# Two experts at a time, each in a piece of 2048 and a piece of 1536 columns, with the routing sums and the decay rows made in another way

## The chip, the cores and the metric

The kernel runs on one core of a Trainium2 chip. Its engines are TensorE (PE, with its weight loads listed apart as PEld), VectorE (DVE), ScalarE (ACT), GpSimd (POOL) and SyncE (SP), which here only issues the transfers of weights. The metric is the device time of one execution in microseconds; the median of three executions counts.

## The reference, cut to what matters

Two layers on 256 tokens of 1024 channels, all in fp32. Each layer mixes tokens in three ways (convolution, Mamba-2 state space, attention), then has a feed-forward part: dense in layer 0, eight experts of which each token takes two in layer 1.

```python
SEQ, D_MODEL, FFN_EXPERT, N_EXPERTS, MOE_TOPK = 256, 1024, 3584, 8, 2

def _swiglu(h, wg, wu, wd):
    return (jax.nn.silu(h @ wg) * (h @ wu)) @ wd

def _moe(h, router_w, router_b, wg, wu, wd):
    logits = (h @ router_w + router_b).astype(jnp.float32)
    top_v, top_i = lax.top_k(logits, MOE_TOPK)
    top_w = jax.nn.softmax(top_v, axis=-1)
    gates = jnp.sum(top_w[..., None] * jax.nn.one_hot(top_i, N_EXPERTS, dtype=jnp.float32), axis=-2)
    ...
    for e in range(N_EXPERTS):
        out = out + gates[..., e:e + 1] * _swiglu(h, wg[e], wu[e], wd[e])
    return out

# in _ssd: 16 heads, two chunks of 128 tokens; a_cum is the running sum of dt * a
    seg = a_cum[..., :, None] - a_cum[..., None, :]
    lmat = jnp.where(causal, jnp.exp(jnp.where(causal, seg, 0.0)), 0.0)
    y_diag = jnp.einsum('bgrcls,bcsgrp->bclgrp', cb[:, :, None] * lmat, xdt)
    y_off = jnp.einsum('bclgn,cbgrpn,bgrcl->bclgrp', cr, prev, jnp.exp(a_cum))
```

## The kernel before, in words

Weights never stay in the chip. SP copies them from DRAM in units of 1 MB (128 partitions of 8 KB) into slots of SBUF, PE waits for a slot's semaphore, and SP refills a slot when PE has counted its last use. Every product is fp32, and one product in the program is two MATMUL records in the profile.

**The experts.** Before the loop the kernel routes: it takes the two best experts of each token, counts tokens per expert, and puts the tokens of each expert side by side (`xg_all`). Expert 0 comes first, because its 14 units are loaded before the counts are known; the other seven follow by count: the largest, the smallest, the second largest, and so on (`ranks`, `places`). An expert has 7 groups of 512 of its 3584 hidden columns, and a group has 6 units: two of gate, two of up, two of down, so 42 units in all and 336 for the eight experts. `expert_load` puts unit u in slot u mod 14, and may issue it when `unit_s` says that the unit 14 places back is consumed. So loads run at most 14 units ahead of PE.

Each engine runs the same loop (`expert_loop`) with its own branch into one of six forms, made for up to 32, 64, 96, 128, 160 and 256 tokens. In the forms up to 128 tokens the tokens are the stationary operand and the weights stream through; above it the weights are stationary. In a form the order is gate of group g, then the turned hidden rows of group g-1, up of group g, perhaps one of four `token_step`s, down of group g-1. A token_step either gathers late tokens (expert 0) or scatters a quarter of the last expert's output back to all tokens and adds it. On PE the last products of a form stand in a common tail (`finish`), where the next form's code is also asked for ahead by branch hints. After an expert ACT copies its output from PSUM into `ysb`; DVE copies the next tokens into `xg`.

**The decay loop** (`lmat_exp`, `seg_of`, `lmat`, `y_batch`). In the last eight of a layer's 32 projection chunks (`w_next`, 16 products each) a batch k of four heads and one chunk is worked in between. PE multiplies a broadcast column by a triangle, which puts the running sums of four heads on all 128 partitions of a PSUM bank (`acum_bcast(k+1)`, line 766), and then multiplies the finished batch (`y_batch(k)`). DVE subtracts and takes the minimum with 0 (four instructions, line 1730), ACT takes the exponential, DVE multiplies it (lines 1738 and 1739), and PE uses it one chunk later. In layer 0 GpSimd multiplies modulation weights at the same time.

**The routing.** PE makes per-expert sums in `token_sums` (line 1037), DVE makes a 0/1 matrix of places from them, and PE gathers the first 256 places by 16 products (line 1055) through two banks that DVE empties by turns, doing one step of the ordering after each. ACT copies the first expert's tokens on.

## Time and profile before

| | |
|---|---|
| median of 3 runs | 1940.09 us (1939.89 to 1940.14) |
| profiled execution | 1941.03 us, its span 1939.3 us |
| PE busy | 1816.8 us, 94% of the span |
| DVE, ACT, POOL busy | 479.1, 272.9, 353.6 us |
| read from DRAM | 531.60 MB |
| chain that ended last | PE 80%, SP's queue 9%, DMA 7% |

The span is cut into 40 slices of 48.5 us. Slices 22 and on are the experts. The chain that ended last goes through PE where PE never waits, and through SP's queue and DMA where a weight unit is what PE waits for. A timeline row gives start, duration, engine, line, tile written and tiles read, count of merged records, and in brackets the idle time before with what ended it.

### The profile page before, as it was taken

The page shows a single profiled execution, that of the slowest core. Times are in us where ns is not written, and L with a number is a line of the kernel's source. Part 1 is how long each engine was busy: PE and PEld are TensorE (multiplying, and loading weights), DVE is VectorE, ACT ScalarE, POOL GpSimd, SP SyncE. Part 2 cuts the span into 40 slices and gives each one's busy share as a digit, 9 for nine tenths or more (in the row PEclk, how much of TensorE's full clock was granted, in tenths as well). Part 3 has the DMA queues.
Part 4 walks back from the last instruction along what each step waited for, and adds up shares of the span by engine and source line. Part 5 has one row for each costly group of instructions (what it writes and reads, how often), then busy time and mean ns, then how long its engine had stood idle before and what let it go on. Part 6 is the DMA issues. An engine that isn't in the chain of part 4 may idle for free.

```text
span 1939.3 us, 28677 instructions
## 1 busy us (share of the span) xinstructions
PE 1816.8 (94%) x11479; PEld 1320.5 (68%) x11480; DVE 479.1 (25%) x1074; ACT 272.9 (14%) x519; POOL 353.6 (18%) x215
## 2 busy tenths in 40 slices
PE   7999999999999999999988799997999969999887
PEld 5888888878888788888865487763344425555433
DVE  1694474110001392433232000101000110001001
ACT  2104312010000202423021000010000100010101
POOL 2707291079996000000000000000000000000000
PEclk8999999999999999999989799999899989999999
DMA  9745364266773544333458986579998899999996
GB/s 399 259 153 203 118 235 149 85 271 244 269 275 132 192 152 145 116 109 109 174 217 362 420 347 261 234 272 421 420 422 308 339 421 419 419 418 420 420 420 280
DMA packets 74009, 534.69 MB, mean 276 GB/s; under 512 B 8336, under 2 KB 8336, under 8 KB 9104
## 3 DMA queue, kind: packets, MB, share of 16 engines
q1 hardware_dynamic: 67824, 490.24, 64.2%
q0 software_dynamic: 5760, 41.95, 5.8%
q8 instruction: 108, 1.77, 0.4%
q10 hardware_dynamic: 288, 0.50, 0.1%
q14 instruction: 29, 0.24, 0.0%
HBM read 531.60 MB, written 1.05 MB: 275 GB/s over the span
## 4 chain that ended last, share of the span: by engine, by line
PE 80%; SPq 9%; DMA 7%; ACT 1%; issue 1%; DVE 1%; DVEq 0%; ACTq 0%
PE ps L708 22%; PE ps L1142 11%; SPq L531 8%; PE ps L794 8%; PE ps L811 7%; PE ps L1290 6%; PE ps L1180 5%; PE ps L818 4%; PE ps L1310 3%; DMA xc<-in_moe_units 3%; PE ps L1220 2%; DMA sq<-in_moe_units 2%; DMA ring<-in_moe_units 1%; PE ps L1251 1%; DMA misc<-in_ada_units 1%
## 5 line engine op out<-in xcount | busy, mean ns | idle before, releaser
L708 PE MATMUL ps<-hT,ring 128*128 128x256 f32 x1984 | 437.8, 381 | 1.0 <-ACT hT L1417 1.0
L708 PEld LDWEIGHTS ps<-hT,ring 128*128 128x128 f32 x1984 | 376.4, 191 | 54.7 <-issue 3.8
L625 POOL TENSOR_TENSOR aring<-aring,ccol 128x2048 f32<-128x2048 f32 x40 | 144.5, 3613 | 212.0 <-ACT hT L1417 98.6
L631 POOL TENSOR_TENSOR aring<-aring 128x1024 f32<-128x1024 f32 x80 | 151.5, 1894 | 6.3
L811 PE MATMUL ps<-hT,ring 128*128 128x256 f32 x672 | 146.7, 379 | 0.0
L1142 PE MATMUL ps<-ring,hT 128*64 128x256 f32 (+2 forms) x1144 | 132.3, 362 | 7.4 <-DMA ring<-in_moe_units 6.7
L811 PEld LDWEIGHTS ps<-hT,ring 128*128 128x128 f32 x672 | 127.0, 190 | 16.9
L2087 DVE TENSOR_TENSOR proj<-proj,ps 128x256 f32<-128x256 f32 (+2 forms) x28 | 14.6, 521 | 413.9 <-PE ps L1142 413.9
L1142 PEld LDWEIGHTS ps<-ring,hT 128*64 128x64 f32 (+2 forms) x1144 | 75.0, 132 | 60.0 <-issue 35.9
L1795 DVE SCALAR_TENSOR_TENSOR misc<-cpad,par,misc 128x256 f32<-128x256 f32 x240 | 102.7, 506 | 0.0
L1422 ACT ACTIVATE proj<-ps 128x512 f32<-128x512 f32 x64 | 38.2, 597 | 339.2 <-PE ps L708 326.2
L794 PE MATMUL ps<-proj,ring 128*128 128x256 f32 x384 | 83.4, 379 | 0.0
L794 PEld LDWEIGHTS ps<-proj,ring 128*128 128x128 f32 x384 | 72.8, 190 | 10.0
L818 PE MATMUL ps<-proj,ring 128*128 128x256 f32 x352 | 77.8, 379 | 0.0
L818 PEld LDWEIGHTS ps<-proj,ring 128*128 128x128 f32 x352 | 66.8, 190 | 9.0
L1546 ACT ACTIVATE proj<-ps 128x256 f32<-128x256 f32 (+2 forms) x28 | 13.0, 464 | 366.3 <-PE ps L1142 366.3
L1290 PE MATMUL ps<-hT,ring 128*128 128x160 f32 x416 | 61.0, 303 | 1.1 <-DMA ring<-in_moe_units 1.1
L1908 DVE TENSOR_TENSOR proj<-proj,ps 128x256 f32<-128x256 f32 x22 | 9.3, 421 | 204.6 <-ACT proj L1520 204.6
L1290 PEld LDWEIGHTS ps<-hT,ring 128*128 128x128 f32 x416 | 58.3, 192 | 2.2 <-DMA ring<-in_moe_units 1.4
L794 PE MATMUL ps<-hT,ring 128*128 128x256 f32 x256 | 55.6, 379 | 0.0
L1220 PE MATMUL ps<-ring,hT 128*32 128x256 f32 x624 | 44.8, 421 | 10.4 <-DMA ring<-in_moe_units 9.7
L794 PEld LDWEIGHTS ps<-hT,ring 128*128 128x128 f32 x256 | 48.6, 190 | 6.6
(373 smaller groups left out, 2005.2 us busy)
## 6 DMA issues: line engine op xcount, KB each, us to landing
ring<-in_moe_units SPq DMA_DIRECT2D x144, 1024.0 KB, 22.1
ring<-in_dense_units SPq DMA_DIRECT2D x121, 1024.0 KB, 4.9
aring<-in_moe_units SPq DMA_DIRECT2D x48, 1024.0 KB, 21.0
proj<-in_moe_units SPq DMA_DIRECT2D x48, 1024.0 KB, 20.7
aring<-in_ada_units POOLq DMA_DIRECT2D x40, 1024.0 KB, 6.0
extra<-in_moe_units SPq DMA_DIRECT2D x24, 1024.0 KB, 21.8
xc<-in_moe_units SPq DMA_DIRECT2D x24, 1024.0 KB, 22.4
misc<-in_moe_units SPq DMA_DIRECT2D x24, 1024.0 KB, 22.9
```

What stands on the lines that cost most here:

```text
L531: sp.dma_start(eslot[u % EXP_SLOTS], moe_units[ds(expert, 1), u].rearrange("e p n -> p (e n)")).then_inc(efull[u % EXP_SLOTS], 16)
L625: last = g.tensor_tensor(w, w, ccol[:, :].unsqueeze(2).broadcast_to([P, KT, 256]), ALU.mult)
L631: last = g.tensor_tensor(dst, w[:, 0:half_k, :], w[:, half_k:2 * half_k, :], ALU.add)
L708: last = mm(ps[:, n % 2, j * SEQ:(j + 1) * SEQ], wide(s)[:, k, j * P:(j + 1) * P], hT[:, k, :], start=(k == 0), stop=(k == KT - 1))
L794: last = mm(ps[:, idx % 2, j * SEQ:(j + 1) * SEQ], view(s)[:, k, (cols + j) * P:(cols + j + 1) * P], rhs[:, k, :], start=(k == 0), stop=(k ...
L811: last = mm(ps[:, j, c0:c0 + n], wide(w)[:, k, j * P:(j + 1) * P], x_src[:, k, 0:n], start=(k == 0), stop=(k == KT - 1))
L818: last = mm(ps[:, 2 + m // 2, (m % 2) * SEQ:(m % 2 + 1) * SEQ], rows2(slot)[:, j, m * P:(m + 1) * P], hm[:, b, j, :], start=(first and j = ...
L1142: last = mm(ps[rows * c:rows * (c + 1), bank, 4 * t0:4 * (t0 + rows)], xg[:, 4 * h + k, t0:t0 + rows], w[:, k, 4 * rows * c:4 * rows * (c ...
L1180: last = mm(dst, hmt[:, g % 2, h0:h0 + rows], w[:, i, cols], start=(g == 0 and j == 0), stop=(g == GE - 1 and j == 3))
L1220: last = mm(ps[r0:r0 + n, bank, 0:SEQ], xg[:, 4 * h + k, 0:n], w[:, k, SEQ * c:SEQ * (c + 1)], start=(h == 0 and k < 2), stop=(h == 1 and ...
L1290: last = mm(ps[:, j % 2, c0:c0 + n], w[:, k, j * P:(j + 1) * P], xg[:, 4 * h + k, 0:n], start=(h == 0 and k == 0), stop=(h == 1 and k == 3))
L1795: v.scalar_tensor_tensor(cacc[:, m, :], cpad[:, m, ds(k, SEQ)], cwcol[:, l, ds(k * CT + m, 1)], cacc[:, m, :], ALU.mult, ALU.add).then_inc ...
```

## The change: pairs of experts in pieces, and two ways of making sums

The loop runs over four pairs. Each pair is worked in four pieces, in the order of `HALVES`: groups 0 to 3 of the first member (24 units), groups 0 to 3 of the second, groups 4 to 6 of the first (18 units), groups 4 to 6 of the second. In pairs the places of the order are (expert 0, largest), (smallest, second largest) and so on. All four engines branch for each piece, SP loads the units in this order, and the 14 slots stay. The code of each form now exists once for each piece. ACT writes the output of a first piece to `ysb[member]`, and after the second piece DVE adds the new output to it (`add_y`). Scattering the pair before's second member is done in piece 0, the first member's in piece 3 (`MID_STEP`, `END_STEP`). `xg` is filled anew for each piece.

In the decay loop `acum_bcast` and `seg_of` go. PE makes the running sums with heads on partitions by two products, DVE copies them to `acum_t`, ACT stores them to DRAM and reads them back, spread over 128 partitions (`spread_rows`), one batch ahead. Four Relu on ACT take the place of DVE's four subtractions.

In the routing the sums are two products, the gather writes into four banks without a wait, ACT copies the tokens straight from PSUM, and DVE does its ordering steps in one go.

```diff
+CUT = (0, 4, GE)
+HALVES = ((0, 0), (1, 0), (0, 1), (1, 1))
+PAIRS = EXPERTS // 2
+MID_STEP = ({2: 2}, {}, {}, {1: 1, 2: 3})
+END_STEP = ({0: 0, 1: 1, 2: 3}, {}, {}, {0: 0, 1: 2})
...
+def half_units_order(half):
+    order = []
+    for i in range(CUT[half + 1] - CUT[half]):
+        order += [("g", i, 0), ("g", i, 1), ("u", i, 0), ("u", i, 1)]
+        if i:
+            order += [("d", i - 1, 0), ("d", i - 1, 1)]
+    return order + [("d", i, 0), ("d", i, 1)]
...
+        order = half_units_order(half)
+        groups = CUT[half + 1] - CUT[half]
+        out.append(Piece(member, half, groups, {key: n for n, key in enumerate(order)}, len(order), unit, group, index))
+        unit, group = unit + len(order), group + groups
...
+        ysb = [part.rearrange("p (t a) n -> p t (a n)", t=TT) for part in (proj[:, 8:16, :], scan[:, 8:XT + 4, :])]
...
-        def count_after(eng, e):
+        def expert_after(piece, p):
+            return p * 2 + (1, 0, 1, 2)[piece.index]
+        def count_after(eng, piece, p):
             eng.wait_ge(ord_s, 1)
-            return eng.value_load(cnt[0:1, ds(e + 2, 1)], min_val=0, max_val=SEQ)
+            return eng.value_load(cnt[0:1, ds(expert_after(piece, p) + 1, 1)], min_val=0, max_val=SEQ)
...
+            def pair_loads(members, p):
+                for piece in PIECES:
+                    for u in range(piece.units):
+                        stream = piece.first_unit + u
+                        if stream < EXP_SLOTS:
+                            continue
+                        sp.wait_ge(unit_s, p * (2 * UNITS) + (stream - EXP_SLOTS + 1))
+                        expert_load(members[piece.member], piece.half, u, stream)
...
-            def acum_bcast(l, k):
-                hb, cc = k // 2, k % 2
-                if k >= 2:
-                    pe.wait_ge(lm_s, 8 * l + k - 1)
-                for r in range(4):
-                    h = 4 * hb + r
-                    last = mm(ps[:, 3 + k % 2, r * P:(r + 1) * P], dts[:, 4, cc, h:h + 1].broadcast_to([P, P]),
-                              triu[:, :], start=True, stop=True)
-                last.then_inc(bc_s, 1)
...
-                mm(ps[:, 2, 368:384], ones[:, :], dts[:, 4, 0, :], start=True, stop=True).then_inc(ac_s, 1)
+                mm(ps[:, 2, 368:384], ones[:, :], dts[:, 4, 0, :], start=True, stop=True)
+                for cc in range(TT):
+                    last = mm(ps[0:HEADS_S, 2, cc * P:(cc + 1) * P], dts[:, 4, cc, :], triu[:, :], start=True, stop=True)
+                last.then_inc(ac_s, 1)
...
-            token_sums(0, lower + [(striu, mask[:, 0, :])])
-            token_sums(8, lower + [(ones, mask[:, 0, :]), (striu, mask[:, 1, :])])
-            token_sums(16, lower)
-            token_sums(24, [(ones, mask[:, t, :]) for t in range(TT)]).then_inc(cum_s, 1)
+            mm(ps[:, 1, 0:4 * EXPERTS], ones[:, :], rt[:, 14:16, :, :].rearrange("p i t e -> p (i t e)"),
+               start=True, stop=True)
+            mm(ps[:, 1, 0:2 * EXPERTS], striu[:, :], rt[:, 12, :, :].rearrange("p t e -> p (t e)"),
+               start=False, stop=True, skip_group_check=True).then_inc(cum_s, 1)
...
             for m in range(KT):
-                if m >= 2:
-                    pe.wait_ge(cf_s, CF0 + KT + m - 1)
                 for t in range(TT):
                     pe.wait_ge(p_s, t + 1)
-                    last = mm(ps[:, 6 + m % 2, 0:SEQ], h_tm[:, t, m, :], p_early[:, t, :],
+                    last = mm(ps[:, 4 + m // 2, (m % 2) * SEQ:(m % 2 + 1) * SEQ], h_tm[:, t, m, :], p_early[:, t, :],
                               start=(t == 0), stop=(t == TT - 1))
                 last.then_inc(c_s, 1)
...
+                def mid_group(i):
+                    if i in MID_STEP[index]:
+                        token_step(MID_STEP[index][i])
+                def end_group(i):
+                    if i in END_STEP[index]:
+                        token_step(END_STEP[index][i])
+                    elif i == 0:
+                        pe.wait_ge(ye_s, p * 4 + index)
+                    elif index == 3:
+                        x_rows_early()
...
+                def spread_rows(k):
+                    hb, cc = k // 2, k % 2
+                    rows = acum_rows[l, 4 * hb:4 * hb + 4, cc * P:(cc + 1) * P].unsqueeze(0).broadcast_to([P, 4, P])
+                    act.dma_start(seg[:, cc, :, :], rows).then_inc(rows_in[cc], 16)
+                    if cc:
+                        act.dma_start(cdec[:, :, :], rows).then_inc(cdec_in_s, 16)
                 def lmat_exp(k):
+                    hb, cc = k // 2, k % 2
+                    act.wait_ge(rows_in[cc], 16 * (4 * l + hb + 1))
+                    for r in range(4):
+                        last = a_(seg[:, cc, r, :], seg[:, cc, r, :], ACT.Relu, scale=-1.0,
+                                  bias=acum[:, cc, 4 * hb + r:4 * hb + r + 1])
+                    last.then_inc(seg_s, 1)
+                    if cc:
+                        act.wait_ge(cdec_in_s, 16 * (4 * l + hb + 1))
+                        a_(cdec[:, :, :], cdec[:, :, :], ACT.Exp)
                     act.wait_ge(seg_s, 8 * l + k + 1)
-                    if k % 2:
-                        a_(cdec[:, :, :], ps[:, 3 + k % 2, :].rearrange("p (a b) -> p a b", a=4), ACT.Exp)
-                    a_(seg[:, k % 2, :, :], seg[:, k % 2, :, :], ACT.Exp).then_inc(ls_s, 1)
+                    a_(seg[:, cc, :, :], seg[:, cc, :, :], ACT.Exp, scale=-1.0).then_inc(ls_s, 1)
...
+                    if i >= 6:
+                        act.wait_ge(y_s, 8 * l + i - 5)
+                        spread_rows(i - 4)
...
+                        act.wait_ge(row_out_s, 16 * (l + 1))
+                        act.wait_ge(pv_s, HEADS_A * (l + 1))
+                        for k in range(2):
+                            spread_rows(k)
...
-                act.wait_ge(unit_s, E0 + UNITS)
-                if n <= HALF:
-                    a_(ysb[:, 0, 0:512], ps[:, 2, :], ACT.Copy).then_inc(ye_s, 1)
-                else:
-                    evac_y(n)
+                            after = count_after(act, piece, p)
+                    act.sem_inc(esil_s, GS)
+                    act.sem_inc(ehte_s, GS)
+                    act.sem_inc(qsil_s, GS)
+                if piece.half == 0:
+                    act.wait_ge(unit_s, E0 + piece.units)
+                    evac_y(n, ysb[piece.member])
...
+            for i in range(KT // 2):
+                act.wait_ge(c_s, KT + 2 * i + 2)
+                a_(xg[:, 2 * i:2 * i + 2, :], ps[:, 4 + i, :].rearrange("p (a b) -> p a b", a=2),
+                   ACT.Copy).then_inc(xg_s, 2)
...
+            for step in steps_between:
+                step()
+            for i in range(KT // 2):
+                dve.wait_ge(xg_s, 2 * i + 2)
+                v.tensor_copy(xg_all[:, 2 * i:2 * i + 2, 0:SEQ], xg[:, 2 * i:2 * i + 2, :]).then_inc(cf_s, 2)
...
+            def add_y(n, y):
+                if n <= HALF:
+                    last = v.tensor_tensor(y[:, 0, 0:512], ps[:, 2, :], y[:, 0, 0:512], ALU.add)
+                else:
+                    for t0, rows in token_blocks(n):
+                        for c in range(max(2, P // rows)):
+                            src, cols = y_bank(t0 // P, t0 % P, rows, c)
+                            dst = y[t0 % P:t0 % P + rows, t0 // P, cols]
+                            last = v.tensor_tensor(dst, src, dst, ALU.add)
+                last.then_inc(ye_s, 1)
...
+                if piece.index == 3:
+                    matrix()
+                if piece.half:
+                    dve.wait_ge(unit_s, E0 + piece.units)
+                    add_y(n, ysb[piece.member])
```

The next rows are what ACT executes in the decay loop for a batch with an even and one with an odd number. Before, with `heads` the tile that holds the differences and `L1422` the copy of a projection chunk:

```order
L1422 ACTIVATE proj<-ps 128x512
L1480 ACTIVATE heads<-heads 128x512
L1422 ACTIVATE proj<-ps 128x512
L1479 ACTIVATE heads<-ps 128x512
L1480 ACTIVATE heads<-heads 128x512
```

And now (`L1479` is the copy of the chunk, `L1540` and `L1542` are the reads from DRAM, `L1548` the Relu):

```order
L1479 ACTIVATE proj<-ps 128x512
L1540 DMA heads<-acum_rows 128x4x128
L1542 DMA heads<-acum_rows 128x4x128
L1548 ACTIVATE heads<-heads,acum 128x128 x4
L1555 ACTIVATE heads<-heads 128x512
L1479 ACTIVATE proj<-ps 128x512
L1540 DMA heads<-acum_rows 128x4x128
L1548 ACTIVATE heads<-heads,acum 128x128 x4
L1553 ACTIVATE heads<-heads 128x512
L1555 ACTIVATE heads<-heads 128x512
```

Each batch has gained the reads for the next batch and four instructions ahead of its exponentials.

On PE the routing was, from the sums (`L1037`) over the gather (`L1055`) to the rows of places (`L1064`):

```order
L677 MATMUL ps<-stk,heads 128x8 x2
L1037 MATMUL ps<-heads,ones 128x8 x2
L1037 MATMUL ps<-heads,striu 128x8
L1037 MATMUL ps<-heads,ones 128x8 x3
L1037 MATMUL ps<-heads,striu 128x8
L1037 MATMUL ps<-heads,ones 128x8 x4
L1055 MATMUL ps<-proj 128x256 x16
```

and is now, in the same place:

```order
L1076 MATMUL ps<-heads,ones 128x32
L1078 MATMUL ps<-heads,striu 128x16
L1088 MATMUL ps<-proj 128x256 x16
L1097 MATMUL ps<-ident,token_slot 128x128 x4
L1097 MATMUL ps<-ident,token_gate 128x128 x4
```

Eleven products for the sums have become two; the 16 products of the gather are the same in number and size.

## Rows read from the trace of the kernel before

**Rows 1.** Page, part 2: transfer rate in 40 slices of 48.5 us.

```profile
GB/s 399 259 153 203 118 235 149 85 271 244 269 275 132 192 152 145 116 109 109 174 217 362 420 347 261 234 272 421 420 422 308 339 421 419 419 418 420 420 420 280
```

**Rows 2.** Busy time by stretch of the expert loop; columns in its first line.

```profile
core 0: us, PE busy (x) PEld busy (x) DVE busy (x) ACT busy (x) POOL busy (x), PEclk, DMA share, GB/s
...
1107.00:1297.00 190.00, 188.76 (x1240) 147.71 (x1242) 15.19 (x41) 10.10 (x31) 0.00 (x0) 0.99 0.70 278
...
1377.00:1529.00 152.00, 151.24 (x392) 67.43 (x394) 9.64 (x18) 9.91 (x17) 0.00 (x0) 1.00 0.93 362
...
1608.00:1736.00 128.00, 123.36 (x1721) 70.83 (x1717) 8.91 (x18) 10.50 (x20) 0.00 (x0) 1.00 1.01 419
...
sum 902.00, PE 820.32 PEld 465.26 DVE 81.50 ACT 70.30 POOL 0.00; mean PE 74.57 PEld 42.30 DVE 7.41 ACT 6.39 POOL 0.00
```

**Rows 3.** Chain in order of time, expert loop: start us, us, what.

```profile
1150.02 17.58 PE ps L1290 x128
...
1168.24 9.26 PE ps L1310 x48
...
1302.41 1.03 PE ps L1240 x8
1303.44 1.86 PE ps L1220 x32
...
1307.96 1.85 PE ps L1251 x16
...
1397.98 6.87 PE ps L1142 x16
...
1405.48 7.06 PE ps L1180 x16
...
1625.51 5.49 PE ps L1142 x96
...
1632.41 5.74 PE ps L1180 x48
```

**Rows 4.** Timeline of PE at two changes of expert; idle before in brackets.

```profile
1292.49 3.70 PE L1310 MATMUL ps<-sq,proj 128*128 128x512 f32 x8 [1.24 <-issue]
...
1305.97 1.99 PE L1088 MATMUL ps<-proj 128*128 128x256 f32 x8 [0.66 <-issue]
...
1730.44 1.94 PE L1180 MATMUL ps<-misc,proj 128*64 128x512 f32 x8 [1.37 <-issue]
...
1736.23 3.67 PE L1142 MATMUL ps<-aring,hT 128*64 128x256 f32 x32 [2.14 <-issue]
```

**Rows 5.** Page, part 6: DMA issues, KB each, us to landing.

```profile
ring<-in_moe_units SPq DMA_DIRECT2D x144, 1024.0 KB, 22.1
ring<-in_dense_units SPq DMA_DIRECT2D x121, 1024.0 KB, 4.9
...
aring<-in_ada_units POOLq DMA_DIRECT2D x40, 1024.0 KB, 6.0
```

**Rows 6.** Timeline of PE in the decay loop of layer 1.

```profile
842.13 7.17 PE L708 MATMUL ps<-hT,ring 128*128 128x256 f32 x32
849.14 1.05 PE L766 MATMUL ps<-triu,dts 128*128 128x128 f32 x8
```

**Rows 7.** Timeline of DVE in the decay loops, layer 0 and then layer 1.

```profile
263.05 2.83 DVE L1739 TENSOR_TENSOR heads<-heads,cbm 128x512 f32<-128x512 f32 x1
...
859.31 1.13 DVE L1730 TENSOR_SCALAR heads<-ps,acum 128x128 f32<-128x128 f32 x4 [5.05 <-PE ps L766]
861.62 0.69 DVE L1738 TENSOR_TENSOR heads<-heads,xc 128x512 f32<-128x512 f32 x1 [1.18 <-ACT heads L1480]
```

**Rows 8.** Timeline of PE in the routing.

```profile
1003.00 1.02 PE L1037 MATMUL ps<-heads,ones 128*128 128x8 f32 x4 [3.23 <-DVE heads L1944]
...
1009.63 9.98 PE L1055 MATMUL ps<-proj 128*128 128x256 f32 x32 [1.76 <-DVE proj L1957]
...
1021.97 1.26 PE L1220 MATMUL ps<-aring,hT 128*32 128x256 f32 x17 [0.58 <-issue]
```

More of the change, by code:

```diff
@@ L15 @@
 from concourse import mybir
+from collections import namedtuple
 from contextlib import ExitStack
@@ L99, in trunk @@
     ORDER, PLAN, LAST, FILLS = ring_plan()
-    UNIT, AT = expert_units()
+    PIECES = pieces()
     ctx = ExitStack()
@@ L466, in expert_loop @@
[L466 removed]
+            last, end = f"{tag}_last", f"{tag}_end"
+            heads_, tails = ([f"{tag}_{what}{piece.index}" for piece in PIECES] for what in ("head", "tail"))
             if finish is not None:
                 block_start(eng)
[L469 to L485 removed]
@@ L494, in expert_loop @@
-            for size, at in places.items():
-                to_form[size].branch_hint(at)
-            for n in SIZES:
-                with nc.body(f"{tag}_{n}", valid_engines=own):
-                    ahead = eng.mark_branch_hint_location()
-                    after = expert(n, e, before)
-                    nc.regs_mov(past, count)
-                    nc.regs_mov(now, after)
-                    nc.regs_mov(done, e)
-                    nc.regs_add(index, index, 1)
-                    if finish is None:
-                        eng.br_lt(index, EXPERTS, on_true=head, on_false=f"{tag}_{n}_last").branch_hint(ahead)
-                    else:
-                        eng.br_lt(index, EXPERTS + 1, on_true=tail, on_false=f"{tag}_{n}_last").branch_hint(ahead)
-                with nc.body(f"{tag}_{n}_last", valid_engines=own):
-                    if finish is not None:
-                        block_start(eng)
+            eng.br(heads_[0])
@@ L511, in expert_loop @@
+            if finish is not None:
+                with nc.body(f"{tag}_over", valid_engines=own):
+                    block_start(eng)
                     eng.br(last)
+            for i, places in hints:
+                for size, at in places.items():
+                    to_form[i][size].branch_hint(at)
             with nc.body(last, valid_engines=own):
```

441 lines of the change are left out of this document (233 added, 208 removed).

## The prediction

> **What bounds the kernel now.** I read the page's transfer rates in slices first, then busy time by stretch of the expert loop, then the chain in order of time for the price of each group, then the timelines at the joints. Transfers run flat at about 420 GB/s in most slices of the experts, and fall to 261 and 234 in slices 25 and 26 and to 308 and 339 in slices 31 and 32 [rows 1]. Those dips are where PE works for many tokens: 278 GB/s with PE busy for 188.76 of 190 us (expert 1, 160-token form), 362 GB/s with 151.24 of 152 us (expert 3, 128) [rows 2]. In the other stretches PE waits for units: over the whole loop it is busy 820.32 of 902 us [rows 2]. So two limits take turns: a large expert holds the slots full and SP may not load, a small one then has at most 14 units in hand, empties them and waits. One load is 1.049 MB, which at 420 GB/s takes 2.50 us; the 322 loads behind the first 14 need 805 us, and the loop takes 902. What is lost by full slots is 190 x (1 - 278/420) = 64 us in expert 1 and 152 x (1 - 362/420) = 21 us in expert 3, together 85 us [rows 2]. Up to layer 1's routing PE is the bound, with the weights prefetched.
>
> **Part 1, the pairs.** It moves no bytes and removes no product; it changes only who is behind whom. I walk through the pieces. A piece has n units, PE needs T for it, and S units are loaded ahead when it starts. Loads possible are T/2.50, but no more than n + 14 - S; the rest of the time the queue idles.
> T comes from groups [rows 3]: 32-token form 1.03 + 2 x 1.86 + 1.85 = 6.6 us; 160-token form 17.58 + 9.26 = 26.84; 128-token form 2 x 6.87 + 7.06 + about 0.6 for the turn = 21.4; 96-token form 2 x 5.49 + 5.74 + about 0.45 = 17.2. A token_step costs 1.99 us when rows of the 160-token expert are scattered [rows 4]; I take the same for the late gather, and 0.6 to 1.1 for others. At a joint the waits that PE has there now are kept: 1.24 and 0.66 us in one, 1.37 and 2.14 us in the other [rows 4]; I use 2.2 for the small form, 1.4 for 160, 0.7 for 128 and 4.2 for 96.
> Pair 0: small 4 groups, T = 26.4 + 8.0 + 2.2 = 37 us: 14.8 loads, S goes 14 -> 4.8. Large 4 groups, 109 us: room for 33.2 loads = 83 us, idle 26 us, S = 14. Small 3 groups, 22 us: S = 4.9. Large 3 groups, 85 us: room for 27.1 = 68 us, idle 17 us. Pair 1: small, S = 4.8; 128-token 4 groups, 86 us: idle 3 us; then 22 us and 67.5 us: idle 0. Pair 2: 33 us, S = 3.3; the 96-token piece of 73 us leaves S = 8.6; from the next small piece on PE waits for units, and the rest runs at the transfer rate, as experts 5 to 7 do now (419 GB/s in rows 2).
> Idle 46 us in place of 85: **39.5 us gained** if each piece end costs what an expert end costs now. It will not quite: eight pieces end before the transfers take over, where four experts do now, and beyond the waits counted above each has a new branch, a copy of tokens to `xg` and, every second time, DVE's addition of up to six instructions. The copy and the addition lie under the next piece's first two products of gate and up (3.8 us in the small form); the addition is nearest to DVE's 0.69 us for 512 columns [rows 7], so about 3 us for six, just covered. I take 0.7 us a piece over for the code, 5.5 us. Bounds: 0, if each piece end costs no more than what I kept, and 28 us (3.5 a piece, the 1.37 and 2.14 of rows 4). Part 1 is -34 us, between -40 and -12. It can't be more than 902 - 820 = 82 us.
>
> **Part 2, the decay loop.** It removes eight `acum_bcast` in each layer, a merged record of 1.05 us each [rows 6], 0.07 of it beside the next one. PE never waits there: a chunk (7.17 us, rows 6) starts as soon as the batch is done, so each counts, 7.8 us a layer. The last one is given back, as PE then waits for DVE's gate products behind ACT anyway, and two small new products cost 0.5. What must stay hidden: after `y_batch(k-1)` ACT issues the reads for k+1, does four Relu and one or two exponentials of 512 columns, and DVE multiplies; PE is ready again after one chunk, 6.9 us. No Relu of 128 x 128 stands in the trace; the nearest is DVE's subtraction, 1.13 us for four [rows 7], taken as it is; an exponential I take at 0.7 like DVE's 0.69 for 512 columns, an issue at 0.35. Layer 1: 0.1 + 0.7 + 1.1 + 1.4 + 2 x 0.69 = 4.7 us, hidden, so -6.4. Layer 0: while GpSimd works, a multiplication takes 2.83 us and not 0.69 [rows 7], so an odd batch has 0.1 + 0.35 + 1.1 + 1.4 + 5.7 = 8.6 us against 7.4 with the transposes: about 1.2 us late at three of eight, and half a microsecond in all for the first reads, so -2.1 to -3. The reads themselves: 256 KB in pieces of 512 bytes, which no row shows; the nearest are 1 MB loads that land in 4.9 us (dense) and 6.0 us (modulation) [rows 5]. They are issued one batch, some 8 us, before they are used. I take 5 us: hidden. The upper bound is the 22.1 us of a full queue [rows 5]. Part 2 is -8.5 us, between -14 and, were landing 15 us, +25.
>
> **Part 3, the routing.** The sums run from 1003.0 us to about 1007.9 in 11 products; two cost about 0.9, so -4.0. The gather takes 9.98 us for 16 products of 256 columns [rows 8]; a chunk does 16 of the same size in 6.9 us [rows 6], so -3.0. DVE has three more small steps ahead, +0.4. DVE's ordering steps, some 4.8 us, end before the gather does. PE starts the experts at 1021.97 [rows 8]; SP's loads start with it: **-6.5 us**, between -3 and -8, and it passes whole, since both limits shift.
>
> **Sum** against the profiled execution: 1941.0 - 34 - 8.5 - 6.5 = 1892. The median of the runs lies 0.9 below that execution, so **1891 us**.
>
> **Rivals.**
> *A, the joints.* Each piece end costs 3.5 us more than now. For it: PE "issue" waits of 1.24, 1.37 and 2.14 us stand at the ends of two experts, where PE has all its data [rows 4]. Against: the next code is asked for ahead. Part 1 falls to -12: 1913. The Trainium skill has a rule for it ("Runtime: NRT & Kernel Launch", Instruction fetch mechanics): code is streamed in sequence, and a taken branch out of the window stalls for a fetch; the trace agrees so far that waits without a data cause stand at branches, but it does not show a fetch.
> *B, the chain in layer 0 and the reads.* DVE's slow multiplications or reads that land in 8 to 10 us eat all of part 2 and some more: with +1 in place of -8.5, 1900. For it: DVE's 2.83 us against 0.69 [rows 7]. Against: rates in the layers are 100 to 250 GB/s [rows 1].
> *C, slower than before.* Reads land as in a full queue, 22.1 us [rows 5]. A batch's buffer is free only after `y_batch(k-2)`, so two batches last landing + 4.7 us in layer 1 and landing + 9 in layer 0, against 15.7 and 16.5 now available. At 22 us that is 11 and 14.5 us for each of 3.5 pairs: +89 in place of -8.5, 1989. It decides for slower from a landing of 15 us on. Against: the queue is not full there.
> *D, more than forecast.* Joints cost nothing over (PE stays busy, and its clock with it): 1884.
>
> **How the numbers follow.** Forecast and D together 0.72 (1880 to 1899), A 0.15, B 0.08, C 0.03, 0.02 for what I don't see. Eight in ten: from 1879 to 1914, which takes in A. A measurement of this kernel tells about 0.2% (4 us) from no change. Faster by more 0.94, within 0.02, slower 0.04.
>
> **What would show it.** Rates by slice: the dips at slices 25, 26, 31 and 32 gone; in the experts' stretches idle queue time near 46 us, all in pairs 0 and 1. PE in pair 0 without a wait for DMA. Joints: "issue" waits of at most 2 us between pieces; 4 or more would be A. In the decay loops chunks follow batches without gap in layer 1 and with gaps of about 1 us at odd batches in layer 0; PE waiting for DVE there by more would be B, ACT waiting for the reads C. First product of the experts 6.5 us nearer to the last product of the router. I am wrong if the transfers reach 420 GB/s in pairs 0 and 1 (another bound), or if the slots run empty in pair 0.

## The result: 31 us slower, and the profile after

The changed kernel takes 1970.99 us (median of 4 runs, 1969.96 to 1971.62), the kernel before beside it 1940.12 us; the ratio is 1.0157, with a 95% interval of 1.0141 to 1.0173. Its profiled execution has a span of 1968.1 us. I had forecast 1891 us. The sign was wrong, and the time lies outside my range of 1879 to 1914.

First the parts that went about as foreseen. The decay loop of layer 0 (timeline of PE, then of DVE and ScalarE; idle before in brackets):

```profile
265.15 0.64 PE L822 MATMUL ps<-heads,proj 128*64 128x128 f32 x4 [2.84 <-DVE heads L1813]
...
284.69 0.45 PE L822 MATMUL ps<-heads,proj 128*64 128x128 f32 x4 [1.23 <-DVE heads L1813]
```

```profile
257.73 4.61 DVE L1812 TENSOR_TENSOR heads<-heads,scan 128x512 f32<-128x512 f32 x1 [2.41 <-ACT heads L1555]
262.27 2.82 DVE L1813 TENSOR_TENSOR heads<-heads,cbm 128x512 f32<-128x512 f32 x1
```

```profile
255.27 1.28 ACT L1548 ACTIVATE heads<-heads,acum 128x128 f32<-128x128 f32 x4 [0.41 <-PE ps L822]
256.55 0.63 ACT L1553 ACTIVATE heads<-heads 128x512 f32<-128x512 f32 x1
```

Four Relu take 1.28 us, an exponential 0.63, and PE is late at two odd batches, by 2.84 and 1.23 us (I had counted three, of 1.2). The reads that no row of before could price (DMA issues of the changed kernel; KB each, us to landing):

```profile
heads<-acum_rows ACTq DMA_DIRECT2D x24, 256.0 KB, 5.8
```

In layer 1 no chunk waits, and the records of 1.05 us between them are gone [rows 6]. The last convolution product behind the loop starts at 898.58 us, against 904.58 before: part 2 brought 6.0 us (rows of before, then of after).

```profile
904.58 3.69 PE L794 MATMUL ps<-misc,ring 128*128 128x256 f32 x16 [1.04 <-DVE hT L1865]
```

```profile
898.58 3.69 PE L837 MATMUL ps<-misc,ring 128*128 128x256 f32 x16 [1.51 <-DVE hT L1939]
```

The routing of the changed kernel, to be laid beside [rows 8]:

```profile
998.84 0.41 PE L1076 MATMUL ps<-heads,ones 128*128 128x32 f32 x2 [3.71 <-DVE heads L2021]
...
1001.40 9.39 PE L1088 MATMUL ps<-proj 128*128 128x256 f32 x32 [1.76 <-DVE proj L2034]
...
1012.96 1.93 PE L1279 MATMUL ps<-aring,hT 128*32 128x256 f32 x32 [0.38 <-issue]
```

From the sums to the gather it is now 2.56 us, before 6.63. The gather itself, 9.39 us against 9.98, hardly moved. The experts start at 1012.96 us, 9.0 us earlier than in [rows 8]. Of the 6.0 us of part 2 only 4.2 are left when the sums start (998.84 against 1003.00 us). The other 1.8 us go in the stretch just ahead, where PE is busy for 18.66 us with as many records as took 17.30 before, at a granted clock of 0.93 against 0.96 (rows of before, then of after):

```profile
980.00:1003.00 23.00, 17.30 (x89) 11.31 (x87) 9.67 (x34) 9.53 (x17) 0.00 (x0) 0.96 0.82 342
```

```profile
974.00:998.84 24.84, 18.66 (x89) 11.51 (x87) 10.09 (x37) 9.52 (x17) 0.00 (x0) 0.93 0.85 349
```

Such a row gives, after the bounds of the stretch: its length, busy time and count of PE, PEld, DVE, ACT and POOL, the granted clock as a share of 2.4 GHz, the DMA share and GB/s.

The loss is in the experts. Waits of PE in the changed kernel's expert loop, 1012 to 1953 us (us in total, times, longest):

```profile
PE ps L1202 <- issue: 49.0, 9, 8.9
PE ps L1240 <- issue: 17.1, 8, 5.2
PE ps L1310 <- DVE proj L2219: 8.3, 6, 4.0
PE ps L1348 <- issue: 8.3, 2, 4.9
PE ps L1368 <- issue: 7.6, 2, 4.6
```

"issue" is idle time for which the profile shows no releaser: it names no data and no semaphore that was late. The rows that answer to [rows 4], joints between pieces:

```profile
1053.74 2.50 PE L1348 MATMUL ps<-hT,proj 128*128 128x160 f32 x8 [4.87 <-issue]
...
1162.88 5.39 PE L1368 MATMUL ps<-ring,proj 128*128 128x512 f32 x8 [4.58 <-issue]
...
1331.05 6.66 PE L1202 MATMUL ps<-proj,hT 128*128 128x512 f32 x8 [5.12 <-issue]
...
1757.49 5.04 PE L1202 MATMUL ps<-aring,hT 128*64 128x256 f32 x32 [8.87 <-issue]
```

In [rows 4] such waits were 0.66 to 2.14 us. Here 17 of them are of 2.5 to 8.9 us, 79.4 us in all. L1348 and L1202 are the first product of a form, right behind the jump from a tail to it; L1368 (down, in its tail part) stands behind the jump from a form to its tail. Each joint has both jumps.

What PE waits for shows in the DMA view. Queue 8 carries instructions, each packet 16,384 bytes. In the wait before 1053.74 us, 1048.9 to 1053.7, it has one packet, and so it has in the next one, 1158.3 to 1162.9:

```profile
q8 instruction: 1, 0.02, 1.4%
```

```profile
q8 instruction: 1, 0.02, 1.3%
```

The first ends at 1051.92 us, 1.8 before PE goes on, the second at 1160.88, 2.0 before. Of all 17 waits every one ends 1.6 to 2.2 us after the end of such a packet, whatever its own length (2.5 to 8.9 us).

Transfers and the granted clock in 40 slices of 49.2 us, and the queues that carry instructions:

```profile
PEclk9999999999999999999988999999989999989999
...
GB/s 395 256 150 214 150 260 150 126 224 276 270 252 174 129 152 147 122 177 130 185 284 418 290 243 401 260 317 420 323 418 344 353 419 418 418 287 419 418 419 212
...
q8 instruction: 145, 2.38, 0.5%
q14 instruction: 98, 0.80, 0.1%
```

The same two queues of the kernel before:

```profile
q8 instruction: 108, 1.77, 0.4%
...
q14 instruction: 29, 0.24, 0.0%
```

The dips did not go [rows 1]: they are there again at other places, now because PE stands still and its slots stay full. 2.38 MB in 145 packets of queue 8 are 16.4 KB each. The changed kernel reads 37 packets more than the one before.

The table adds up all waits of PE in the expert loop by releaser (rows of the waits view) beside PE's busy time and granted clock (windows view). The experiments below are in it too.

```
                          loop us  PE busy  issue   DMA   DVE   ACT  PEclk
before                      904     821.7    10.9  65.0   2.6   3.4   0.97
changed                     941     828.4    92.2   3.3   8.3   8.1   0.94
changed, no hints          1039     853.1   172.5   1.1   5.2   5.8   0.89
before, not aligned         929     834.8    35.6  49.8   2.6   2.1   0.94
before, no hints            929     830.9    44.8  48.1   2.6   2.1   0.95
pieces in turn              974     845.0    76.1  40.3   5.2   5.4   0.92
aligned, tail first         909     823.3    36.6  29.1  11.7   8.1   0.96
tails aligned               908     820.9    50.0  17.4  10.2   8.6   0.96
aligned, no idle padding    889     810.5    18.1  42.2   9.5   8.3   0.98
aligned pieces in turn      935     831.9    20.4  72.5   5.2   4.7   0.96
aligned, all engines        879     810.2    15.6  39.0   5.9   7.9   0.97
```

Changed less before is +37 us of loop: issue +81.3, DVE +5.7, ScalarE +4.7, busy time +6.7, and DMA -61.7. So the pairs did take away the waits for weights, and paid for them with more in waits for code.

### The profile page after: what moved, and what is told of

It reads as the page before. It is cut to its first block, busy times and chain, and to the rows that moved or that the text cites. A ratio compares the mean times of both kernels' runs of the same rounds, so it can differ in the third digit from the quotient of the medians.

```text
span 1968.1 us, 28770 instructions
## 1 busy us (share of the span) xinstructions
PE 1809.5 (92%) x11341; PEld 1316.3 (67%) x11342; DVE 479.2 (24%) x1038; ACT 286.3 (15%) x575; POOL 353.9 (18%) x215
## 3 DMA queue, kind: packets, MB, share of 16 engines
q8 instruction: 145, 2.38, 0.5%
HBM read 537.89 MB, written 1.08 MB: 274 GB/s over the span
## 4 chain that ended last, share of the span: by engine, by line
PE 84%; issue 5%; DMA 5%; ACT 2%; DVE 2%; SPq 1%; DVEq 0%; ACTq 0%
PE ps L762 21%; PE ps L1202 14%; PE ps L837 8%; PE ps L854 7%; PE ps L1240 7%; PE ps L1348 6%; PE ps L861 4%; PE ps L1368 3%; PE ps L1279 3%; DMA ring<-in_moe_units 2%; PE ps L1310 2%; DMA misc<-in_ada_units 1%; DMA proj<-in_moe_units 1%; SPq L577 1%; PE ps L773 1%
## 5 line engine op out<-in xcount | busy, mean ns | idle before, releaser
L762 PE MATMUL ps<-hT,ring 128*128 128x256 f32 x1984 | 437.7, 381 | 1.0 <-ACT hT L1474 1.0
L762 PEld LDWEIGHTS ps<-hT,ring 128*128 128x128 f32 x1984 | 376.6, 191 | 56.0 <-issue 5.1
L854 PE MATMUL ps<-hT,ring 128*128 128x256 f32 x672 | 146.7, 379 | 0.0
L854 PEld LDWEIGHTS ps<-hT,ring 128*128 128x128 f32 x672 | 127.0, 190 | 16.9
L1202 PE MATMUL ps<-ring,hT 128*64 128x256 f32 (+2 forms) x800 | 95.8, 374 | 8.7 <-issue 8.5
L1202 PEld LDWEIGHTS ps<-ring,hT 128*64 128x64 f32 (+2 forms) x800 | 53.9, 136 | 46.6 <-issue 31.3
L1479 ACT ACTIVATE proj<-ps 128x512 f32<-128x512 f32 x64 | 38.2, 597 | 314.5 <-PE ps L762 300.1
L1202 PE MATMUL ps<-proj,hT 128*64 128x256 f32 (+2 forms) x336 | 52.9, 433 | 31.6 <-issue 31.6
L1240 PE MATMUL ps<-ring,proj 128*64 128x512 f32 (+2 forms) x336 | 73.8, 532 | 6.8 <-issue 3.4
L1202 PEld LDWEIGHTS ps<-proj,hT 128*64 128x64 f32 (+2 forms) x336 | 27.3, 158 | 58.9 <-issue 54.8
L1202 PE MATMUL ps<-aring,hT 128*64 128x256 f32 (+2 forms) x464 | 53.9, 366 | 8.9 <-issue 8.9
L1240 PEld LDWEIGHTS ps<-ring,proj 128*64 128x64 f32 (+2 forms) x336 | 25.4, 138 | 47.7 <-issue 44.0
## 6 DMA issues: line engine op xcount, KB each, us to landing
misc<-in_moe_units SPq DMA_DIRECT2D x24, 1024.0 KB, 16.4
```

The source lines that it names most:

```text
L762: last = mm(ps[:, n % 2, j * SEQ:(j + 1) * SEQ], wide(s)[:, k, j * P:(j + 1) * P], hT[:, k, :], start=(k == 0), stop=(k == KT - 1))
L854: last = mm(ps[:, j, c0:c0 + n], wide(w)[:, k, j * P:(j + 1) * P], x_src[:, k, 0:n], start=(k == 0), stop=(k == KT - 1))
L1202: last = mm(ps[rows * c:rows * (c + 1), bank, 4 * t0:4 * (t0 + rows)], xg[:, 4 * h + k, t0:t0 + rows], w[:, k, 4 * rows * c:4 * rows * (c ...
L1240: last = mm(dst, hmt[:, g % 2, h0:h0 + rows], w[:, i, cols], start=(g == 0 and j == 0), stop=(g == GS - 1 and j == 3))
```

## What the experiments tell apart

Theory 1: PE waits for its own instructions behind jumps. The change doubles the joints and also moves TensorE's code. In the kernel before the shared tail and five of six forms begin at a multiple of 256 instructions (`block_start`, an alignment of 256 with offset 255, stands ahead of the loop and behind each form); in the changed kernel `block_start` is left only ahead of the first head and at the end. Counted in the built programs, with a slot for each instruction of a block of 256, the four tails begin at slot 117 and reach into the next block, and the forms begin at slots 5 to 254. In the kernel before the tail begins at slot 0 and ends ahead of slot 216. Theory 2: work at the joints (copies, sums, a late count). Theory 3: any jump costs, wherever it lands.

**1. Parts 2 and 3 alone** (`decay_routing_only`). The kernel before with these two diffs:

```diff
-                for k in range(8):
-                    seg_of(l, k)
+                act.dma_start(seg[:, cc, :, :], rows).then_inc(rows_in[cc], 16)
...
-            token_sums(24, [(ones, mask[:, t, :]) for t in range(TT)]).then_inc(cum_s, 1)
+            mm(ps[:, 1, 0:4 * EXPERTS], ones[:, :], rt[:, 14:16, :, :].rearrange("p i t e -> p (i t e)"),
```

> The kernel before with parts 2 and 3 alone (decay rows read back from DRAM and Relu on ScalarE; two routing sums, gather into banks 4 to 7); its expert loop is the old one, whole experts one after the other. The profile of the changed kernel has the first expert product at 1012.96 us against 1021.97 before, so every theory expects about 9 us less than before: 1931 us, between 1928 and 1935. A time above 1937 would mean that these parts cost something inside the expert loop.

1930.5 us against 1941.49, ratio 0.9937 (0.9920 to 0.9953). These parts are a gain of 11 us, as expected.

**2. Part 1 alone** (`pairs_only`): the changed kernel with the old decay loop and routing, the two diffs of experiment 1 turned round.

> The changed kernel with the decay loop and the routing of the kernel before: part 1 alone. If the parts add up, all of the loss and 9 us more lie here: 1980 us, between 1975 and 1985. If the loss came from parts 2 and 3 (code or data that they displace), it would be near 1940.

1975.14 us, ratio 1.0165 (1.0142 to 1.0188). The whole loss lies in the pairs. The parts don't add up exactly (-11 and +34 would make +23, measured +31); the interval of this run is 9 us wide, and I leave that open. The trace has 17 waits of such length here, too, 86.7 us in all.

**3. The pieces in turn** (`pieces_in_turn`):

```diff
-HALVES = ((0, 0), (1, 0), (0, 1), (1, 1))
+HALVES = ((0, 0), (0, 1), (1, 0), (1, 1))
```

with the token steps, the matrix and the next count moved to the pieces where they now belong.

> The changed kernel with the same 16 pieces, but both pieces of an expert in succession (large, large, small, small), so that the reads are again not mixed between a large and a small expert. Theory 1 (each joint costs some 5 us of TensorE's wait for its own code, and mixing large and small experts does give back some 38 us of idle queue): the joints cost the same, the mixing is lost, so about 38 us above the changed kernel, 2000 to 2015. Theory 2 (the cost lies in going from one expert to another at each joint: other tokens, another count, a late copy): half of the joints stay within an expert, so the loss is about halved, 1965 to 1985.

2003.55 us, ratio 1.0317 (1.0300 to 1.0334): 33 us above the changed kernel, within what theory 1 expected. Theory 2's halving is out; with as many joints and no mixing, PE waits 76.1 us for "issue" and 40.3 for weights.

**4. The old layout for the new loop** (`aligned_tail_first`). Same instructions and order; on TensorE only, ahead of each tail and behind each form:

```diff
-                            eng.br(tails[i]).branch_hint(ahead)
+                            eng.br_lt(pair, PAIRS, on_true=tails[i], on_false=f"{form}_{n}_pad").branch_hint(ahead)
+                        with nc.body(f"{form}_{n}_pad", valid_engines=own):
+                            block_start(eng)
+                            eng.br(last)
```

and tail 3 is put ahead of head 0. As in the kernel before, the form that stands right behind a tail and a head (here that of 32 tokens, four of the 24 forms) does not begin at slot 0, but at slot 213 or 217.

> The changed kernel, computing the same in the same order, with only TensorE's code laid out as in the kernel before: every form of a piece and every tail begins at a multiple of 256 instructions, and the tail that ends a pair stands right ahead of the head of the next one. Theory 1 (fetch of code after a jump that lands in the middle of a block of 256): the waits of TensorE without a cause in the data, 93 us in the expert loop, fall to 11 to 25 us and the time to 1890 to 1915. Theory 2 (work at the joints: copies, sums, late count): nothing changes, 1965 to 1975. Theory 3 (any jump costs, wherever it lands): waits stay above 70 us, time above 1950.

1936.26 us, ratio 0.9963 (0.9948 to 0.9978): 35 us came back by layout alone, and the waits without a releaser fall from 92.2 to 36.6 us. Theories 2 and 3 fall. Less came back than I expected, 1890 to 1915; what is left is inside the small pieces, first of all:

```profile
1174.05 1.93 PE L1291 MATMUL ps<-extra,hT 128*32 128x256 f32 x16 [4.00 <-issue]
...
1191.20 1.94 PE L1322 MATMUL ps<-ring,proj 128*32 128x512 f32 x8 [5.10 <-DVE proj L2231]
```

**5. The opposite** (`before_not_aligned`): the kernel before with `block_start` emptied.

```diff
-            eng.addr_align(256, offset=255, max_nops=0)
+            return
```

> The kernel before, same instructions in the same order, only without the alignment ahead of its shared tail and behind each of its six forms, so that the tail lies across a multiple of 256 instructions and the forms begin at slots 95 to 184 of such a block, as in the changed kernel. Theory 1 (where a jump lands decides): with 8 joints, each with 4 to 5 us of TensorE's wait that has no cause in the data on one or both of its two jumps, 1965 to 2010 us. Theory 3 (the number of jumps decides, not where they land): no change, 1938 to 1945.

1968.31 us, ratio 1.0136 (1.0119 to 1.0152). The old kernel, with its 8 joints, gets the same waits, seven of 3.2 to 5.0 us, each ending 1.5 to 3.1 us after a packet of queue 8:

```profile
1296.72 3.77 PE L1310 MATMUL ps<-sq,proj 128*128 128x512 f32 x4 [4.44 <-issue]
...
1624.01 8.51 PE L1142 MATMUL ps<-aring,hT 128*64 128x256 f32 x96 [3.91 <-issue]
...
1743.73 5.54 PE L1180 MATMUL ps<-proj 128*64 128x512 f32 x24 [5.00 <-issue]
```

**6. Without hints** (`before_no_hints`, and at the end `changed_no_hints`). The calls that name the next jump ahead of time are left out:

```diff
-eng.br_lt(index, EXPERTS + 1, on_true=tail, on_false=f"{tag}_{n}_last").branch_hint(ahead)
+eng.br_lt(index, EXPERTS + 1, on_true=tail, on_false=f"{tag}_{n}_last")
...
-            for size, at in places.items():
-                to_form[size].branch_hint(at)
```

> The kernel before with its alignment, but without the hints that name the next jump ahead of time, on all engines. Theory 1: each of 8 joints then has two jumps whose code is read only when they are taken, 4 to 5 us each: 60 to 80 us slower, 2000 to 2020, which bounds what a joint can cost. If hints did nothing here, 1941.

1967.57 us, ratio 1.0136 (1.0119 to 1.0153). Hints are worth 26 us there, less than half of what I gave them: waits of 3.7 to 6.6 us come, but partly take the place of waits for weights (65.0 to 48.1 us).

> The changed kernel without the hints that name the next jump, on all engines, its layout otherwise as it is. Taking them away cost the kernel before 26 us over 8 joints. If in the changed kernel the hints still do their part, 16 joints without them cost 40 to 52 us more: 2010 to 2025. If the unaligned tails and forms have already made them nearly useless (theory 1: the wait is there with or without the hint), it stays within 15 us of the changed kernel: 1965 to 1986. I expect the second.

2066.6 us, ratio 1.0641 (1.0624 to 1.0659). **Both expectations missed.** The hints still save the changed kernel some 96 us. Without them nearly every jump shows, form to tail and tail to form:

```profile
1050.60 1.94 PE L1296 MATMUL ps<-stk,proj 128*128 128x64 f32 x8 [5.94 <-issue]
...
1062.15 2.50 PE L1345 MATMUL ps<-hT,proj 128*128 128x160 f32 x8 [5.12 <-issue]
...
1174.29 5.84 PE L1365 MATMUL ps<-ring,proj 128*128 128x512 f32 x8 [7.37 <-issue]
```

Summed by row there are 30 waits above 0.9 us, 170 us; the 28 above 2.4 us end 1.2 to 3.6 us after a packet of queue 8. With hints the first of these is 0.50 us in the changed kernel, the second 4.87. So the hints there covered one jump of a joint and left the other open; it is not, as I expected, that they had become useless.

**7. Tails alone aligned** (`tails_aligned`): as 4, with a pad only behind the last form of a piece.

```diff
+                        if finish is not None and n == SIZES[-1]:
```

> The changed kernel with only the four tails (and the heads right behind them) at a multiple of 256 instructions, the forms where they fall. If the tail across a boundary is what makes both jumps of a joint wait, the time is that of the fully aligned layout, 1930 to 1940; if the start of the forms is, it stays at 1960 to 1971; if both share it, 1945 to 1955.

1934.18 us, ratio 0.9962 (0.9948 to 0.9976), the same as 4. The tail lying across a boundary is what cost the time. Where the forms begin did not change the time, though it did change the waits: PE has 50.0 us of "issue" and 17.4 for weights here, 36.6 and 29.1 in experiment 4, so that one took the place of the other.

**8. Padding inside the forms.** Each form has one more alignment in its last group, so that its end lies in one block. In experiment 4 that jump came at slot 20 (piece 2, 32 tokens) and slots 3 and 16 (64 tokens), just after a new block was entered. First it is put one product later (`aligned_late_padding`):

```diff
-                        if g == GS - 1 and n != 96:
+                        late = n == 96 or (n == HALF and index != 2)
+                        if g == GS - 1 and not late:
```

> The fully aligned layout, with the padding inside three kinds of forms put one product later (piece 2 of 32 tokens: from slot 20 to slot 86; pieces 0 and 3 of 64 tokens: from slots 3 and 16 to 68 and 81). In the aligned layout seven waits of 1.6 to 4.2 us are left, 22 us in all, which would be jumps over padding taken right after a new block was entered. Theory 1: they go, 1936 to 1915 to 1922. If they have another cause: 1933 to 1938.

1926.21 us, ratio 0.9925 (0.9909 to 0.9942): 10 us, between the two expectations, as new waits of up to 3.54 us came behind the late padding. Then it is left out where the end fits into its block anyway (`aligned_no_idle_padding`):

```diff
-                        if g == GS - 1 and n != 96:
+                        if g == GS - 1 and n != 96 and (index, n) not in FITS:
```

> The aligned layout without the inner padding wherever the end of a form fits into the block that it has begun anyway (12 of 24 forms, the 32-token form of piece 2 and the 64-token forms of pieces 0 and 3 among them), so that no jump over padding is taken just after a block was entered, and none is taken late either. Theory 1: the waits inside the small pieces (1.93 and 3.41, 2.63 and 3.13, 2.26 and 1.41, 3.54 us in the version with late padding) go, some 15 us of them: 1912 to 1922. If the late padding had already got what there is to get: 1924 to 1929.

1919.17 us, ratio 0.9894 (0.9878 to 0.9911): within what theory 1 expected. No wait of PE above 2.4 us without a releaser is left.

**9. VectorE and ScalarE too** (`aligned_all_engines`): each piece's head begins at a multiple of 256 on these engines as well.

```diff
-            if finish is not None:
-                block_start(eng)
+            block_start(eng)
```

> The version before this one, with the pieces of VectorE and ScalarE begun at a multiple of 256 instructions too. In the aligned layout these two engines still have waits without a cause in the data of 5 to 10 us (ScalarE 9.9 at 1058, VectorE 6.1 at 1190 and 7.0 at 1203), of which TensorE sees some 8 us. Theory 1 (every engine waits for its own code where its jump lands across a block): VectorE's and ScalarE's waits shrink, and the time falls by a further 3 to 10 us. Rival: on these engines TensorE's lead hides it; within 2 us of the version before it.

1912.94 us, ratio 0.9864 (0.9847 to 0.9880): 6 us more, within what theory 1 expected, and 1.4% faster than the kernel before, the best of all. What DVE did in the version before (`aligned_no_idle_padding`) and does now, at its copy of tokens for the second large piece and at a multiplication that did not change:

```profile
1180.96 1.23 DVE L2181 COPY hT<-proj 128x2048 f32 x1 [6.19 <-issue]
...
1193.42 0.32 DVE L2258 TENSOR_TENSOR proj<-proj,ps 128x160 f32<-128x160 f32 x1 [6.50 <-issue]
```

```profile
1172.98 1.23 DVE L2182 COPY hT<-proj 128x2048 f32 x1 [1.55 <-issue]
...
1186.53 0.32 DVE L2259 TENSOR_TENSOR proj<-proj,ps 128x160 f32<-128x160 f32 x1 [6.88 <-issue]
```

**10. What mixing is worth once joints are cheap** (`aligned_pieces_in_turn`): experiments 3 and 8 together.

```diff
-HALVES = ((0, 0), (1, 0), (0, 1), (1, 1))
+HALVES = ((0, 0), (0, 1), (1, 0), (1, 1))
```

> The aligned layout with the pieces of an expert in succession. If mixing large and small experts gives back the idle queue whatever the joints cost, it is 28 to 40 us slower than the aligned version in pairs (1945 to 1960). If the 32 us between the two unaligned versions were only the joints' different cost, the two aligned versions are within 5 us of each other.

1960.58 us, ratio 1.0106 (1.0089 to 1.0122): 41 us slower than its partner in pairs, `aligned_no_idle_padding` (1919.17), a little more than I expected of the mixing. PE waits 72.5 us for weights in turn, 42.2 in pairs. (The forms whose inner padding is left out are chosen anew, by the same rule.) It also shows that more joints cost something when they are cheap: against the kernel before beside it, it is 20 us slower, where parts 2 and 3 with the old loop (experiment 1) are 11 us faster. So cutting the experts into 16 pieces costs some 31 us even so, and mixing has to earn that back first.

## Why the prediction was wrong

**What bounds.** Right, and confirmed by experiment 10: a large expert fills the slots, a small one empties them. In the aligned version (`aligned_all_engines`) the rates are near what I had looked for:

```profile
GB/s 399 254 154 196 149 284 168 85 255 270 245 275 166 175 147 142 129 154 138 177 242 326 417 227 374 339 304 420 420 409 420 378 420 419 417 418 418 419 418 201
```

Below 420 they are almost only in pair 0 (227, 374, 339, 304 in slices 24 to 27) and in one slice of 378. Against 420 in slices of 47.7 us these five miss 54 us; in [rows 1] slices 24 to 27, 31 and 32 (48.5 us each) miss 8 + 18 + 22 + 17 + 13 + 9 = 87 us. I forecast 85 to 46. So this term of idle queue was about right, 33 us and not 39.5, and it could only be seen once the joints were cheap. It did not become as much time: against the kernel before beside each, that version is 27.4 us faster and parts 2 and 3 alone are 11.0, so the pairs bring some 16 us of the 34 forecast for them.

**Part 1: the step that failed is "I take 0.7 us a piece over for the code, 5.5 us".** The trace has 81.3 us more of "issue" and 10 us more behind DVE and ScalarE. It is not 8 added joints that cost something; shared out over the joints, "issue" is now 92.2/16 = 5.8 us each, where it was 10.9/8 = 1.4 us. My upper bound of 28 us came from the largest joints of before, 1.37 and 2.14 us: a price taken from a layout that the change removes. In the diff `block_start` moves from behind each form to the end of the loop; I passed over it. I had read the hints as cover ("the next code is asked for ahead") and did not ask what makes them reach. Rival A named the mechanism, but I put it at 3.5 us a piece, from the same rows. I also wrote there that the trace does not show a fetch. It can: in the kernel before, a packet of queue 8 ends 0.2 us after the start of the wait of 2.14 us [rows 4], and that wait ends 2.0 us after the packet. The Trainium skill ("Runtime: NRT & Kernel Launch", Instruction fetch mechanics) says that code comes in blocks of 16 KiB, 256 instructions, in sequence, and that a taken branch out of a window of two pages stalls. The runs agree on the block: 16.4 KB a packet, and a tail across the boundary against one inside it is 37 us (experiment 7). The price, 2.5 to 8.9 us a jump in the changed kernel, is from the rows above. The page's sentence that the cost of crossing a boundary is "mostly hidden" agrees with the long pieces here: from 1054 to 1158 us queue 8 has seven packets, and PE has no wait. It does not hold for a jump taken just behind the crossing: the jumps at slots 3 to 20 in experiment 4 came with waits of 2.7 to 4.2 us, and these went in experiment 8.

**The waits cost a second time.** I did not have this at all. The granted clock around the second joint, in PE's wait of 4.58 us and behind it:

```profile
1158.30:1162.90 4.60, 0.02 (x1) 0.02 (x1) 0.00 (x0) 0.00 (x0) 0.00 (x0) 1.00 0.75 274
1162.90:1166.40 3.50, 3.50 (x5) 1.43 (x6) 0.00 (x0) 0.00 (x0) 0.00 (x0) 0.51 0.07 26
1166.40:1170.00 3.60, 3.60 (x41) 1.68 (x43) 0.00 (x0) 1.68 (x4) 0.00 (x0) 1.00 0.16 23
```

It falls from 2.4 to 1.2 GHz as the wait ends, and the first products of the tail take 5.39 us, where they take 3.70 in the aligned kernel. The first joint, 1046 to 1060 us, in the changed kernel and in the aligned one:

```profile
1046.00:1060.00 14.00, 9.09 (x50) 6.78 (x51) 0.00 (x0) 0.60 (x1) 0.00 (x0) 0.63 1.02 415
```

```profile
1046.00:1060.00 14.00, 12.90 (x93) 12.67 (x94) 0.55 (x2) 0.50 (x2) 0.00 (x0) 1.00 1.01 417
```

The eight products that take 1.35 us in the aligned kernel took 2.50. But here the clock is at 0.73 already in 1046 to 1048 us and at 0.50 in 1048 to 1050, so it fell about 2 us before the wait of 4.87 us began, behind waits of 0.50 and 0.86 us that the aligned kernel has too without a fall; why it fell then stays open.

Over the expert loop the trace has the clock at 1.2 GHz in 21 stretches, 119.5 us, in the changed kernel and in 7 stretches, 44.4 us, in the aligned one. PE is busy in 85.3 and 39.1 us of them. At full clock half of that would be saved, so the difference is worth 23 us, and PE's busy time for the same products is in fact 18 us longer, 828 against 810. Without hints the clock is at 1.2 GHz for 232.1 us, PE is busy in 138.1 of them, and its busy time is 853 us.

**Part 2** was -8.5, measured -6.0, within its bounds. The reads landed in 5.8 us, where I took 5. DVE's first multiplication took 4.61 us beside GpSimd, not 2.83 [rows 7], and the first odd batch was late by 2.84 us, not 1.2; four Relu took 1.28, not 1.13. Rivals B and C did not come.

**Part 3** was -6.5, and -3.0 is what the start of the experts shows behind part 2. The sums gave 4.1 us as forecast. The gather gave 0.6 and not 3.0: I priced it by a chunk of the layers, but it runs behind a wait, at a granted clock of 0.50 (changed kernel):

```profile
1001.00:1006.00 5.00, 4.60 (x11) 3.73 (x12) 4.40 (x30) 0.60 (x1) 0.00 (x0) 0.50 0.00 0
```

The start of the experts moved by 9.0 us in all, not 15; the 1.8 us lost ahead of the sums are a term that I did not have.

**The sum** with measured terms: the idle queue -33, parts 2 and 3 -9 to -11, joints +81 + 10, busy time +7, which makes +54 to +56; measured +31. The rest is counted twice: while PE stands still the queue fills the slots, so waits for DMA fell by 61.7 us and not by 33. In the table the waits and the busy time add up to the +37 us of the loop, and the 9 us of its earlier start make it +28, the difference of the two profiled spans. That a stall and a wait for weights cover each other is my reading of these sums; it would also be part of why the hints are worth 26 us in the kernel before, with 8 joints and 65 us of waits for weights to hide behind, and some 96 in the changed one, with 16 joints and 3.3 us.

**Chances.** I gave 0.04 to slower, all of it to a late read. The joint had a chance of 0.15 but a price that could not turn the sign. A code price that no row of before shows needed an upper bound from what happens without its cover, a jump twice a joint. The first run of experiment 6 needs only the kernel before; with its 4 to 7 us a jump the bound would have been some 16 x 10 = 160 us.

## What to carry to other kernels

Splitting a loop body into more pieces multiplies jumps, and what a jump costs depends on where the code lies and on whether it was named ahead: here PE's waits were 0.4 to 1.8 us in the best layout with hints, 2.5 to 8.9 us with the tails across a boundary, and up to 11.2 us without hints, and the clock often fell with them. When a change rewrites a loop that has alignment and hints in it, check that each of them still stands ahead of what it was there for, before pricing the rest; "issue" waits of several microseconds behind a branch are the sign, and a packet of the instruction queue that ends some 2 us before the engine goes on confirms it. The mixing itself is sound: with the tails back inside one block it is 1934.18 us, and 1912.94, 27 us under the kernel before, with two steps that the kernel before does not have (padding left out inside forms, pieces of VectorE and ScalarE aligned). What these two steps would bring to the kernel before was not tried, and 11 of the 27 us are parts 2 and 3.

## What the runs showed that I had not expected

- A 16.4 KB read of instructions is one packet among hundreds and lands in about 1 us (1050.82 to 1051.92 us in the first wait), yet PE stands 2.5 to 8.9 us after a jump that is not covered, and 11.19 us at most without hints. In the changed kernel the last 1.6 to 2.2 us of each such wait come after the packet.
- The granted clock is at half for 119.5 us of the changed kernel's expert loop and for 44.4 us of the aligned one's. At the second joint it fell as a wait of 4.58 us ended; in the aligned kernel, with a wait of 1.08 us there, it stays at 1.00.
- ScalarE stands 9.9 us without a releaser at the first large piece even in the best version; PE waits 0.67 us behind it:

```profile
1055.34 0.50 ACT L1695 ACTIVATE proj<-ps 128x160 f32<-128x160 f32 x2 [9.88 <-issue]
```

- In that wait, 1045.5 to 1055.3 us, the trace has four packets on the other instruction queue, the last 1.5 us before ScalarE goes on:

```profile
q14 instruction: 4, 0.03, 0.8%
```

- That points to code here, too, but no run changed it. Nor was tried the hint for the next form on VectorE and ScalarE, which have none.
